# A two-block layer kernel: the second block's front is reordered and its convolution moves from VectorE to ScalarE and GpSimd

## What is computed

```python
h = rmsnorm(x, norm_mix_g)
q, k, v, qi, ki, wi, glu = split(h @ w_in)          # q 512, k/v/ki 64, qi 256, wi 4, glu 1024 columns
q, k, qi, ki = partial_rope(...)
# for each block of 128 queries: index scores of qi, ki, wi; the 128 best keys are kept
a_out = dsa_attention(q, k, v, qi, ki, wi)
ga, gg = split(glu); u = ga * sigmoid(gg)
u = causal_dwconv(u, conv_b_w, conv_b_b)            # 31 taps a channel, 512 channels
b_out = silu(layernorm(u, ln_b_g, ln_b_b))
x = x + concatenate([a_out, b_out]) @ w_out
hq = rmsnorm(x, norm_cross_g); m = rmsnorm(mem, norm_mem_g)   # cross attention to 256 memory rows
x = x + cross_attention(hq @ w_q, m @ w_k, m @ w_v) @ w_o
hf = rmsnorm(x, norm_ffn_g)
x = x + (silu(causal_dwconv(hf @ w_gate)) * (hf @ w_up)) @ w_down
return rmsnorm(x, norm_final_g)
```

## Time and profile before

| what | us |
|---|---|
| median of 3 runs | 1972.96 (1972.05 to 1974.13) |
| the profiled execution's own time | 1973.02 |
| its span in the profile | 1971.2 |
| TensorE busy | 1785.8 (91%) |
| VectorE, ScalarE, GpSimd busy | 753.3, 392.8, 75.4 |

### The profile page before, as it was taken

How to read it: one execution, slowest core, us unless ns; L and a number is a source line. 1 busy time by engine, 2 the same in 40 slices (tenths; PEclk the granted TensorE clock), 3 DMA queues, 4 the chain that set the end, 5 groups by cost and what they waited for, 6 DMA issues and landing times.

```text
span 1971.2 us, 20259 instructions
## 1 busy us (share of the span) xinstructions
PE 1785.8 (91%) x8038; PEld 907.4 (46%) x8038; DVE 753.3 (38%) x1428; ACT 392.8 (20%) x761; POOL 75.4 (4%) x78
## 2 busy tenths in 40 slices
PE   5997699986899999899899787999999999999997
PEld 4643244442455655444344365453643444444443
DVE  3006534446433333212389868651323222221001
ACT  4032533342111111110101221331311111111000
POOL 0002210000001001000010000000000000000000
PEclk8999899997899999999999888999999999999999
DMA  4211111110011010012222022011111222221212
GB/s 185 96 65 43 43 43 54 43 43 32 33 38 40 23 44 34 33 67 73 91 75 75 22 96 75 35 39 55 43 57 64 81 77 75 75 75 54 85 63 86
DMA packets 33005, 119.74 MB, mean 61 GB/s; under 512 B 3664, under 2 KB 3920, under 8 KB 32528
## 3 DMA queue, kind: packets, MB, share of 16 engines
q1 hardware_dynamic: 31824, 113.78, 16.3%
q10 hardware_dynamic: 864, 3.35, 0.4%
q0 software_dynamic: 224, 1.31, 0.2%
HBM read 116.34 MB, written 2.10 MB: 60 GB/s over the span
## 4 chain that ended last, share of the span: by engine, by line
PE 73%; DVE 16%; issue 6%; ACT 4%; DMA 1%; POOL 0%; ACTq 0%; DVEq 0%; POOLq 0%
PE bank L433 56%; DVE arena L1155 6%; PE vpair L534 3%; DVE tmp L1146 2%; PE abank L507 2%; PE bank L449 2%; PE opair L558 2%; PE abank L649 2%; DVE arena L1563 2%; DVE arena L1146 1%; PE vpair L649 1%; DVE max L1562 1%; PE bank L471 1%; PE abank L518 1%; PE abank L546 1%
## 5 line engine op out<-in xcount | busy, mean ns | idle before, releaser
L433 PE MATMUL bank<-h,ring 128*128 128x512 f32 x1936 | 870.8, 603 | 26.0 <-ACT tmp L916 14.6
L433 PEld LDWEIGHTS bank<-h,ring 128*128 128x128 f32 x1936 | 365.1, 193 | 459.4 <-issue 425.4
L433 PE MATMUL bank<-arena,ring 128*128 128x512 f32 (+1 forms) x1120 | 455.8, 563 | 7.7 <-DVE arena L1146 4.6
L433 PEld LDWEIGHTS bank<-arena,ring 128*128 128x128 f32 x1120 | 210.7, 191 | 225.0 <-issue 206.5
L1155 DVE SCALAR_TENSOR_TENSOR arena<-arena,cols 128x512 f32<-128x512 f32 x168 | 129.7, 772 | 6.0
L1155 DVE SCALAR_TENSOR_TENSOR x<-bank,x 128x512 f32<-128x512 f32 x40 | 27.7, 692 | 258.0 <-PE bank L433 257.6
L899 ACT ACTIVATE arena<-bank 128x512 f32<-128x512 f32 (+1 forms) x72 | 37.6, 523 | 351.4 <-PE bank L433 282.2
L1149 DVE TENSOR_SCALAR arena<-arena,cols 128x512 f32<-128x512 f32 x26 | 14.4, 554 | 223.8 <-ACT arena L1110 219.2
L1146 DVE TENSOR_TENSOR arena<-arena,vpair 128x256 f32<-128x256 f32 x87 | 36.6, 421 | 155.7 <-PE vpair L649 109.6
L507 PE MATMUL abank<-sq,cst 128*128 128x512 f32 (+1 forms) x66 | 39.3, 747 | 55.3 <-ACT sq L871 46.6
L534 PE MATMUL vpair<-arena 128*128 128x256 f32 (+4 forms) x224 | 71.1, 423 | 19.8 <-DVE arena L1146 10.0
(11 more groups left out here) (170 smaller groups left out, 1395.7 us busy)
## 6 DMA issues: line engine op xcount, KB each, us to landing
ring<-weights SPq DMA_DIRECT2D x209, 512.0 KB, 3.2
x<-xt SPq DMA_DIRECT2D x4, 512.0 KB, 7.9
out<-h SPq DMA_DIRECT2D x8, 256.0 KB, 2.0
cst<-cst_in ACTq DMA_DIRECT2D x1, 1504.0 KB, 14.3
arena<-memt ACTq DMA_DIRECT2D x1, 1024.0 KB, 8.0
arena<-mem2t POOLq DMA_DIRECT2D x1, 1024.0 KB, 5.1
tmp<-pos ACTq DMA_DIRECT2D x1, 256.0 KB, 10.5
arena<-wa ACTq DMA_DIRECT2D x1, 256.0 KB, 15.7
```

The source lines that it names most:

```text
L433: last = mm(o[:, 0:n], weight(), src, start=c == 0, stop=c == len(srcs) - 1)
```

## The change

The second block's work is put in another order, and the convolution is taken from VectorE.

- **Norms.** `h` is now `x` times the gain (one `ts1` a tile, in `add_dense`), without the norm's factor. `dense_scaled` starts on that at once: the first group, the total, a second group, then a third on tiles that VectorE has meanwhile scaled. `scaled_start` multiplies the first two groups' outputs by the factor. This stands at all three norms. At the end TensorE adds the last tile's squares itself, and GpSimd scales three of the eight output tiles.
- **Order of the front.** First the two groups of `qi`, then k and ki, then v and wi. The rotations of `qi` and `ki` and the index scores follow, with pairs of twelve other groups (glu 0 and 1, q, glu 2 and 3) between them. The memory's norm is moved into `w_out`. VectorE selects as soon as the index scores are there; in round 6 it breaks off for the rotations of q and k. The weight stream is read in the new order; `w_out_2`'s panels come in two parts.
- **Convolution.** For each tap ScalarE multiplies a shifted `u` by the tap's weight into one of four tiles `cprod`, and GpSimd adds it to the sum in `mix`: 120 products and 120 additions, with four first taps on ScalarE alone. A product waits until the addition four before it is done. `DVE_TILES` is 0, so VectorE has no tap. 36 taps are issued between the groups of the front, the other 88 in sparse attention, five a step.
- **Sparse attention** now carries `cross kv`, four pairs a step. The convolution's mean, variance, factor and gate come in steps 18 to 25, after all additions. `w_out_2` follows as eight whole groups.

```diff
-        stage("glu", *[A8] * 8)
-        stage("sparse", *[A8] * 8)
+        stage("index", V8, V8, A8, A8)
+        stage("front", *[A8] * 12)
...
+        DVE_TILES = 0
+        POOL_TAPS = (TAPS - 1) * (4 - DVE_TILES)
...
+            def dense_scaled():
+
+                dense_normed()
+                norm_total()
+                o = dense_bank()
+                for c in range(KD):
+                    last = mm(o[:, :], weight(), h[:, c, :], start=c == 0, stop=c == KD - 1)
+                    if c < KD - 1:
+                        h_used.inc(last)
+                end_group(last)
+                dense_normed()
...
+                    fill(work)
+            fill(work, 12)
+            pe.wait_ge(dense_act.sem, reads("act", start["front"] + 7))
             for i in range(4):
...
+                single("v", con("rot2"), q2[:, i, :])
+                fill(work, 2)
+            single("v", con("dup0"), kraw)
+            fill(work, 2)
+            single("v", con("rot2dup0"), kraw)
+            finish(work)
...
+            def conv_mean():
+
+                pe.wait_ge(tap_added.sem, POOL_TAPS)
...
-            work = stream([[mix[:, 4 + c, :] for c in range(4)]] * 8)
-            attention(sparse_jobs(), work, 1)
...
+            work = cross_kv()
+            attention(sparse_jobs(), work, (1, 1, 2), {18: conv_mean, 21: conv_variance})
...
+            def taps(n):
+
+                while n and st["tap"] < TAPS * (4 - DVE_TILES):
...
+                        k = st["product"]
+                        if k >= 4:
+                            act.wait_ge(tap_added.sem, k - 3)
+                        do(fn(cprod[:, k % 4], u[:, i, w:w + T], ACT.Copy, scale=weight_), tap_ready)
+                        st["product"] += 1
...
+            after = {i: (lambda: taps(5)) for i in range(18)}
+            after.update({20: conv_squares, 22: conv_rinv, 24: conv_tanh})
...
+            def scaled_start(dst0, dst1):
+
+                ri = rinv_in(0)
+                tt(dst0, dense_in()[:, :], ri, MUL, dense_dve)
+                for i in range(KD - 1):
+                    st["used"] += 1
+                    dve.wait_ge(h_used.sem, st["used"])
+                    tt(h[:, i, :], h[:, i, :], ri, MUL, h_ready)
+                o = dense_in()
+                tt(h[:, KD - 1, :], h[:, KD - 1, :], ri, MUL, h_ready)
+                tt(dst1, o[:, :], ri, MUL, dense_dve)
+                signal_now(norm_applied)
...
-            for i in range(4):
-                dve.wait_ge(u_ready.sem, i + 1)
-                acc = mix[:, 4 + i, :]
...
-                for w in range(1, TAPS):
-                    stt(acc, u[:, i, w:w + T], col("conv_w", i * TAPS + w), acc, MUL, ADD,
...
+                if rnd == 6:
+                    dve.wait_ge(dense_act.sem, reads("act", start["front"] + 7))
+                    for i in range(4):
+                        rope(q2[:, i, :], q2[:, i, :])
+                    rope_dup(kd)
...
+            after.update({19: conv_centre, 23: conv_scale, 25: conv_gate})
+            attention(sparse_jobs(), CROSSKV, [None] * 16, 4, after)
...
+            for k in range(POOL_TAPS):
...
+                pool.wait_ge(tap_ready.sem, k + 1)
+                acc = mix[:, 4 + k // (TAPS - 1), :]
+                do(G.tensor_tensor(acc, acc, cprod[:, k % 4], ADD), tap_added)
```

More of the change, by code:

```diff
@@ L213, in build @@
         sq_hi2 = take(4, T)
+        cprod = take(4, T)
         top[0] = 3 * 2048
@@ L318, in build @@
         GEARLY = stage_groups("gates early", "gates late")
-        OUTB = stage_groups("w_out_2 conv", "w_out_2")
+        CROSSKV = stage_groups("cross kv", "conv norm")
         GLATE = stage_groups("gates late", "gates a")
@@ L471, in dense_tokens @@
                         last = mm(o[:, t * n:(t + 1) * n], src[:, c, tok(t)], w[c][:, 0:n], start=c == 0, stop=c == KD - 1)
-                end_group(last)
+                        if t == tiles - 1 and c == KD - 1:
+                            end_group(last)
+                        if c % 4 == 3:
+                            yield
+            def dense_tokens(src, tiles, n=P):
+                for _ in dense_tokens_pairs(src, tiles, n):
+                    pass
             def other_rows(last):
@@ L520, in _, with attention @@
             att = {"p": 0, "pt": 0}
-            def attention(jobs, work=iter(()), rate=3):
+            def attention(jobs, work=iter(()), fills=(1, 1, 1), after={}):
                 n = len(jobs)
@@ L559, in attention @@
                         o_done.inc(last)
-                    fill(work, 1)
+                    fill(work, fills[2])
+                    if i in after:
+                        after[i]()
             pe.wait_ge(ones_in.sem, 16)
@@ new lines, in _, with cross_kv @@
+            pe.wait_ge(norm_applied.sem, NA + 1)
+            def cross_kv():
+                for n in range(8):
+                    yield from dense_pairs([mem2[:, c, :] for c in range(KD)], M)
+                for n in range(8):
+                    yield from dense_tokens_pairs(mem2, 2)
+            def conv_mean():
+                pe.wait_ge(tap_added.sem, POOL_TAPS)
+                pe.wait_ge(conv_ready.sem, DVE_TILES)
+                o = dense_bank()
+                for i in range(4):
+                    last = mm(o[:, :], con("ones"), mix[:, 4 + i, :], start=i == 0, stop=i == 3)
+                end_group(last)
@@ L805, in _, with conv_variance @@
+            def conv_variance():
+                o = dense_bank()
+                for i in range(4):
+                    pe.wait_ge(squares_ready.sem, i + 1)
+                    last = mm(o[:, :], con("ones"), slot(i), start=i == 0, stop=i == 3)
+                end_group(last)
+            work = cross_kv()
+            attention(sparse_jobs(), work, (1, 1, 2), {18: conv_mean, 21: conv_variance})
+            finish(work)
             pe.wait_ge(mix_ready.sem, 4)
-            work = stream([[mix[:, 4 + c, :] for c in range(4)]] * 8)
@@ L807, in _ @@
-            attention(sparse_jobs(), work, 1)
-            finish(work)
             pe.wait_ge(o_read.sem, state["o"])
             for j in range(8):
-                dense(mix, 4)
-            norm_total()
-            dense_normed()
-            for j in range(7):
+                o = dense_bank()
+                for c in range(KD):
+                    last = mm(o[:, :], weight(), mix[:, (c + 4) % KD, :], start=c == 0, stop=c == KD - 1)
+                end_group(last)
+            dense_scaled()
@@ L815, in _ @@
+            for j in range(5):
                 dense(h)
+            pe.wait_ge(dense_dve.sem, reads("dve", start["cross o"] - 1))
             pe.wait_ge(dense_act.sem, reads("act", start["cross o"] - 1))
@@ L842, in mean_square @@
                 return bufs["att"][0][:, i, :]
-            st = {"dense": 0, "a": 0, "norm": 0, "th": 0, "p": 0, "pt": 0, "gate": 0}
+            st = {"dense": 0, "a": 0, "norm": 0, "th": 0, "p": 0, "pt": 0, "gate": 0, "tap": 0, "product": 0}
             mine = [g for g, (w, _) in enumerate(groups) if w == "act"]
@@ new lines, in _, with conv_squares, conv_rinv @@
+            for i in range(2, 4):
+                glu_gate(i)
+                taps(4)
+                glu_value(i)
+                taps(4)
+            def conv_squares():
+                for i in range(4):
+                    act.wait_ge(conv_ready.sem, DVE_TILES + i + 1)
+                    do(fn(slot(i), mix[:, 4 + i, :], ACT.Square), squares_ready)
+            def conv_rinv():
+                o = dense_in()
+                do(fn(slot(0), o[:, :], ACT.Ln, bias=col("eps6"), scale=1.0 / 512), dense_act)
+                do(fn(slot(0), slot(0), ACT.Exp, bias=col("zero"), scale=-0.5), rinv_ready)
@@ new lines, in conv_tanh @@
+            def conv_tanh():
+                for i in range(4):
+                    act.wait_ge(conv_ready.sem, DVE_TILES + 4 + i + 1)
+                    do(fn(tmp[:, i], mix[:, 4 + i, :], ACT.Tanh, bias=col("ln_b_b", i, of=half), scale=col("ln_b_g", i, of=half)), conv_th)
+            after = {i: (lambda: taps(5)) for i in range(18)}
+            after.update({20: conv_squares, 22: conv_rinv, 24: conv_tanh})
+            attention(sparse_jobs(), CROSSKV,
+                      [lambda n=n: copy_dense(k2[:, n, :], dense_in()[:, 0:M]) for n in range(8)] +
+                      [lambda n=n: copy_dense(v2[:, :, tok(n)], dense_in()[:, 0:M].rearrange("p (s d) -> p s d", s=2)) for n in range(8)],
+                      4, after)
```

271 lines of the change are left out of this document (163 added, 108 removed).

## The result

| | median us (lowest to highest) | profiled execution's span |
|---|---|---|
| before | 1974.13 (1972.05 to 1976.39) | 1971.2 |
| after | 1979.38 (1977.66 to 1980.87) | 1975.7 |

What follows compares the result with a forecast made beforehand. TensorE, busy for 91% of the span, was taken as the bound, so gains lie only where it waits or repeats itself. Terms +16.2-8.3-7.5+0.5=+0.9 us gave 1974.0, own range 1964 to 1984, with rivals 1957 to 1999.

Steps and rivals of the forecast that it cites:

- Norms: At the cross and feed-forward norms, TensorE's early start gains 8.3 and 7.5 us.
- The front, walked through: From `w_out` through index scores to glu groups: last index score on VectorE at 1048, TensorE's products end at 1102.0.
- The selection: VectorE's sixteen rounds, broken by rotations, and masks end at 1132.0, before at 1220.2; TensorE waits some 21 us.
- Attention with taps: Sparse attention: GpSimd sets the pace, 7.0 us a step; 86 additions of 1.40 take 120.4, last at 1255.4.
- The tail: After the last addition: mean at 1262.1, eight steps 21.6 us, VectorE's 11.0 in full, `w_out_2` ends at 1351.4.
- The end: Final norm, second product and split scalings: 0.5 us later, bounded by 1.7 earlier and 2.5 later.
- (1): Convolution's end falls into waits of the tail's steps: front ends 14.3 us earlier, 1960; chance 0.17.
- (2): GpSimd and VectorE hold each other in attention: every addition at 1.67 us, 23 later, 1997; chance 0.17.
- (3): Additions hold VectorE in the selection: attention starts 16 us later, 1990; chance 0.12.
- (4): At the three norms the second group or scaled tiles come late: 25 us back, 1999; chance 0.07.
- the three signs named as wrong: Additions below 1.3 or above 1.5 us; GpSimd, not ScalarE, waiting inside a step; TensorE's clock falling inside the steps.

Runs made afterwards that it cites:

- the old form: Changed kernel with the norms ahead of cross attention and the feed-forward part as before the change: 1995.8 us, 1.0112 to the kernel before.
- both limits were gone: Changed kernel with GpSimd's attention additions on 256 of 512 columns and ScalarE's read-out ahead of the five products: 1958.2 us, 0.9919 to the kernel before.
- half additions: Changed kernel with GpSimd's attention additions on 256 of 512 columns, the rest of the convolution left out there: 1984.0 us, 1.0048 to the kernel before.

## Why the prediction was right, and where it was not

The total was met within 5.4 us, and most steps held; but the step that carried the argument on attention named one limit where there are two.

- **Norms.** +15.8 forecast for two; the old form costs 16.4. From the end of `w_out_2` to the first cross scores 64.9 us became 56.6, 8.3 against 8.3. Right.
- **The front, walked through.** Forecast last index score on VectorE 133.2, seen 137.4. The failed term is "twelve index scores ... 7.7", priced by columns. Two of them, each with the pair behind it:

```profile
1017.41 0.70 PE L557 MATMUL abank<-arena 64*128 64x256 f32 x2
...
1019.95 0.70 PE L557 MATMUL abank<-arena 64*128 64x256 f32 x2
```

These products have 64 rows; a score of 256 columns and a pair follow each other every 2.54 us (1017.41 to 1019.95) where 0.43 and 1.72 make 2.15, and at 384 and 512 columns the excess is 0.39 too. Twelve of them are 4.7 us. The rotations, with 128 rows, cost what was said (4.29 us with two pairs). This is the larger part of the front's error.

- **The selection.** 84.0 us forecast from that point, 84.4 measured. The additions do hold VectorE's rotations (1382 ns for 0.69), but that fell into waits for TensorE.
- **Attention with taps.** 86x1.40=120.4 forecast, 119.0 measured. The number was right, the reason half of it: "ScalarE ... 6.0, TensorE ... 5.5. So GpSimd sets the pace". Adding each engine's work misses the loop over three engines, 6.6 us a step. An addition was 1.34 to 1.35, so GpSimd's true pace was 6.7, and 86 of them without a pause take 116.1; the other 2.9 us are pauses that the loop made. An error in the price (1.40) stood in for the limit that was not seen, and that the sum came out was luck. TensorE's own step was priced too low as well: 5.5 against the 5.93 seen once both limits were gone. A pair took 0.98 us (1197.25 to 1198.23) where 0.86 was counted, and 1271.74-1267.71 less a pair of 1.72 is 2.3, not 2.1.
- **The tail.** 32.6 us forecast from mean to `w_out_2`, 35.9 measured. The term counted VectorE's 11.0 us and left out TensorE's variance (5.07 us in the row at 1274.47); the waits that remain are 2.80+0.83+3.02+0.25+2.84=9.7. The mean itself took 5.2 where 6.7 was counted. So attention and the mean, each 1.4 too long in the sum, hid part of what the scores and the tail lacked.
- **The end.** 0.5 later forecast, 2.1 measured (from the last product of `down`, 1957.4 to 1971.2 before, 1959.8 to 1975.7 after). The second product starts the scalings 1.15 later, the shared scalings take 6.42 us where eight took 6.26, and 3.1 us instead of 2.4 lie behind the last one. It is inside the bounds.

**The rivals.** (1), the convolution's end beside attention, did not happen: the tail has its waits. (2), holding in attention at 1.67 an addition, did not happen: GpSimd kept 1.35 while VectorE paid, its scalings of 128x384 taking 991 ns, 432 with half additions. (3), holding in the selection, did not happen: the row of MAX8 shows 695 ns beside GpSimd, and 695 before; what was held were the two-input products of the rotations (1382 ns), not the one with an input in PSUM (692). The Trainium skill ("SBUF — State Buffer", section "SBUF: two separate sides") gives this rule: VectorE contends with GpSimd only with two SBUF inputs or in a two-port mode, and the one that comes second waits for the other's instruction to end. The trace agrees for these three kinds; in which mode the scalings ran, which were held with one tensor input, no run shows. It agrees on the lock too: the prediction read it as the full 1.26 us for each addition, but it is at most that, 0.69+1.27=1.96 us for a held product, and the longest row is 1.74:

```profile
1082.41 1.74 DVE L1270 TENSOR_TENSOR arena<-tmp 128x512 f32<-128x512 f32 x1
```

(4), a late start at the norms, did not happen.

Of the three signs named as wrong, one came in part. The additions ran between 1.3 and 1.5, and TensorE's clock held in the steps of block 2 (granted 1.00 from 1172 to 1250). But GpSimd waited for ScalarE inside the steps, 2.8 us in all, and ScalarE's products for GpSimd only 1.6 us: this is the loop that the forecast lacked.

## What to carry to other kernels

Where engines hand over in a ring, add the durations along the ring, over as many steps as a buffer spans, before naming the busiest engine as the limit; a read-out that frees a bank should not stand behind work that could follow it. Two limits of nearly the same size hide each other: test them two by two, since the removal of either alone may show nothing or a loss. Here GpSimd's additions cost nothing beside VectorE's maxima and their replacements, and did cost beside products with two SBUF inputs and beside scalings; look at the rows of each kind of instruction before placing such work.

## What the runs showed of the hardware

Beside GpSimd's full additions VectorE's maxima kept their 695 ns, while a scaling of 128x128 rose from 286 to 998 ns and one of 128x384 from 432 to 991 (the lower figures are from the kernel with half additions), and a product of 128x512 with two SBUF inputs from 0.69 to 1.38 us. The scalings end up nearly independent of size, which fits a wait for an addition in progress rather than shared bandwidth. GpSimd itself hardly slowed: 1.33 us an addition beside the maxima of the front, 1.35 in attention, up to 1.48 beside VectorE's taps. A product of 64 rows between products of 128 rows cost 0.39 us more than its columns, at 256, 384 and 512 columns alike. And TensorE's clock fell to 1.2 GHz inside attention behind waits of 2.28 and 3.87 us (granted 0.81 and 0.66 in the stretches above), so that work moved off TensorE did not always shorten its stage.
